# A two-block transformer kernel: small parameter loads put behind the first layer's weights

## The reference, cut to what matters

```python
a = rms_norm(h, attn_norm[i])
proj = a @ w_in[i]                       # queries, keys, values, z, xbc, dt, ...
(da_q, da_k, da_v, ssd_z, ssd_xbc, ssd_dt, gla_q, gla_k, gla_v, gla_g, gla_lr) = jnp.split(proj, IN_SPLITS, axis=-1)
y_da  = diff_attention(da_q, da_k, da_v, positions, da_q_norm[i], da_k_norm[i], ...)
y_ssd = ssd_mixer(ssd_z, ssd_xbc, ssd_dt, ssd_conv_w[i], ssd_conv_b[i], ...)   # xbc is convolved over 4 tokens
y_gla = gla_mixer(gla_q, gla_k, gla_v, gla_g, gla_lr, gla_w_gate2[i], gla_b_gate[i], gla_norm[i])
h = h + concat(y_da, y_ssd, y_gla) @ w_out[i]
f = rms_norm(h, ffn_norm[i])
h = h + (silu(f @ w_ffn_gate[i]) * (f @ w_ffn_up[i])) @ w_ffn_down[i]
h = h + sigmoid(h @ ple_w_gate[i]) * (p[i] @ ple_w_proj[i])
# the second block's modulation, computed during the first block's layers:
mod = silu(c) @ ada_w[i] + ada_b[i]      # and its norm gains norm_pre, norm_post, mla_qa_norm
```

## Time and profile before

| | |
|---|---|
| median of three runs | 1738.55 us |
| the profiled execution's own time | 1739.91 us |
| its span in the profile | 1737.8 us |
| TensorE multiplying | 1689.4 us, 97% of the span |
| VectorE busy | 1185.4 us, 68% |
| ScalarE busy | 905.2 us, 52% |
| GpSimd busy | 41.9 us, 2% |

### The profile page before, as it was taken

One profiled execution on the slowest core, in us unless ns is written; L12 is line 12 of the kernel. 1 busy time (PEld: TensorE's weight loads), 2 busy tenths in 40 slices (PEclk: granted clock), 3 DMA queues, 4 the chain that ended last, 5 costly groups with the idle time before them and its releaser, 6 DMA issues.

```text
span 1737.8 us, 34117 instructions
## 1 busy us (share of the span) xinstructions
PE 1689.4 (97%) x14251; PEld 1462.7 (84%) x14251; DVE 1185.4 (68%) x1656; ACT 905.2 (52%) x1124; POOL 41.9 (2%) x50
## 2 busy tenths in 40 slices
PE   6999999998999999999999999999999989999998
PEld 5977899987987799988888888888888878898896
DVE  4888755537588765546567877768677683687875
ACT  5666433335575443335645545456455562465772
POOL 2000000000000000000000000000000000000130
PEclk9999999999999999999999999999999999999999
DMA  7666778653648756655222322313223123352022
GB/s 199 197 221 257 223 179 200 193 192 130 196 155 306 244 160 181 192 194 170 77 86 62 98 62 62 94 54 98 62 62 98 51 98 134 116 188 79 26 72 99
DMA packets 252857, 241.90 MB, mean 139 GB/s; under 512 B 32932, under 2 KB 212224, under 8 KB 252064
## 3 DMA queue, kind: packets, MB, share of 16 engines
q1 hardware_dynamic: 250896, 233.21, 43.4%
q0 software_dynamic: 1808, 6.50, 1.3%
HBM read 238.61 MB, written 1.08 MB: 138 GB/s over the span
## 4 chain that ended last, share of the span: by engine, by line
PE 82%; DVE 7%; ACT 4%; DMA 3%; DVEq 2%; issue 1%; ACTq 1%; SPq 1%
PE pg L2653 35%; PE pg L1315 34%; PE pm L1315 7%; PE pm L1318 2%; PE pm L2653 2%; DVE ring_r L576 2%; PE pm L2656 1%; DMA ring<-in_w_ffn_up 1%; DVE ring_r L1762 1%; ACT ring_r L569 1%; SPq L2221 1%; DMA ring<-in_hg_w_in 1%; DVEq L1799 1%; DMA ring<-in_w_in 0%; DMA cst<-in_cst 0%
## 5 line engine op out<-in xcount | busy, mean ns | idle before, releaser
L576 DVE TENSOR_TENSOR ring_r<-ring,ring_r 128x2048 fp32r<-128x2048 f32 (+1 forms) x126 | 284.2, 2261 | 170.0 <-ACT ring_r L569 163.8
L2653 PE MATMUL pg<-ring_r,work_r 128*128 128x512 f32 (+1 forms) x1632 | 375.7, 389 | 8.6 <-DVEq L3172 2.7
L2653 PEld LDWEIGHTS pg<-ring_r,work_r 128*128 128x128 f32 x1632 | 299.0, 189 | 77.2 <-issue 10.2
L1315 PE MATMUL pg<-ring_r,work_r 128*128 128x512 f32 (+3 forms) x1280 | 354.6, 383 | 5.5 <-DVE work_r L1768 1.5
L569 ACT ACTIVATE ring_r<-ring 128x2048 fp32r<-128x2048 f32 (+1 forms) x126 | 237.5, 1890 | 200.7 <-DMA ring<-in_w_ffn_up 80.6
L2653 PE MATMUL pg<-work_r,ring_r 128*128 128x256 f32 x2688 | 318.8, 281 | 1.7 <-DVE ring_r L576 1.6
L2653 PEld LDWEIGHTS pg<-work_r,ring_r 128*128 128x128 f32 x2688 | 317.2, 188 | 3.3 <-DVE ring_r L576 2.4
L1315 PE MATMUL pg<-ring_r 128*128 128x512 f32 (+3 forms) x752 | 284.2, 378 | 1.1 <-DVEq L831 1.1
L1315 PEld LDWEIGHTS pg<-ring_r,work_r 128*128 128x128 f32 x1280 | 235.5, 188 | 50.2 <-DVEq L1763 3.5
L1315 PE MATMUL pg<-work_r,ring_r 128*128 128x512 f32 (+1 forms) x976 | 264.4, 360 | 0.0
L1315 PEld LDWEIGHTS pg<-work_r,ring_r 128*128 128x128 f32 x976 | 173.1, 189 | 27.2
(11 more groups left out here) (401 smaller groups left out, 1808.3 us busy)
## 6 DMA issues: line engine op xcount, KB each, us to landing
ring<-in_w_in SPq DMA_DIRECT2D x36, 1024.0 KB, 5.3
ring<-in_hg_w_in SPq DMA_DIRECT2D x48, 512.0 KB, 3.9
ring<-in_w_ffn_gate SPq DMA_DIRECT2D x44, 512.0 KB, 4.0
ring<-in_w_ffn_up SPq DMA_DIRECT2D x44, 512.0 KB, 5.4
ring<-in_w_ffn_down SPq DMA_DIRECT2D x22, 1024.0 KB, 4.9
ring<-in_ada_w SPq DMA_DIRECT2D x16, 1024.0 KB, 8.9
ring<-in_hg_w_in SPq DMA_DIRECT2D x64, 256.0 KB, 3.0
ring<-in_w_out SPq DMA_DIRECT2D x12, 1024.0 KB, 5.7
```

The costliest lines, as they stand in the source:

```text
L576: W.low_done(V.tensor_tensor(lo, W.raw(i, name)[:, 0:lo.shape[1]], W.hi(i, name).bitcast(f32), ALU.subtract))
L1315: return T.matmul(out_, lhsT, rhs, start=first, stop=last)
L2653: return T.matmul(out_, lhsT, rhs, start=first, stop=last)
```

## The change

The convolution's bias and filters move from ahead of piece 4 to behind it, and the row loads move ahead of it. The second norm's gain and the modulation's bias leave the small loads (22 become 20) and are issued behind the layer's last weight piece, on the semaphore of the second half of x, for which ScalarE and VectorE wait ahead of the second norm. GpSimd's five gains of the second block move behind its loads for the first layer.

```diff
-        N_PRM = 22
+        N_PRM = 20
...
                 small_loads = [
-                    (p_convb, cols("ssd_conv_b", i)),
                     (p_qkg[:, 0:DQK], rows("da_q_norm", i)), (p_qkg[:, DQK:], rows("da_k_norm", i)),
...
-                    (p_dskip, rows("ssd_d", i)), (p_ssdn, rows("ssd_norm", i)), (p_glan[:, 0:1], cols("gla_norm", i)),
-                    (p_sub[:, 0:1], cols("da_sub_norm", i)),
-                    (p_ffn, cols("ffn_norm", i)), (p_li, d["lam"][i]),
-                    (p_adab, d["ada_b_2"][i].rearrange("(c p) -> p c", p=P)),
+                    (p_dskip, rows("ssd_d", i)), (p_convb, cols("ssd_conv_b", i)),
                 ]
-                for j in range(4):
-                    small_loads.insert(1 + j, (convw3[:, j, :], d["ssd_conv_w"][i, j].rearrange("(c p) -> p c", p=P)))
+                small_loads += [(convw3[:, j, :], d["ssd_conv_w"][i, j].rearrange("(c p) -> p c", p=P)) for j in range(4)]
+                small_loads += [(p_ssdn, rows("ssd_norm", i)), (p_glan[:, 0:1], cols("gla_norm", i)),
+                                (p_sub[:, 0:1], cols("da_sub_norm", i)), (p_li, d["lam"][i])]
...
+            def load_late_parameters(i):
+                sp.wait_ge(loaded_h[1], 16 + 32 * i)
+                sp.dma_start(p_ffn, cols("ffn_norm", i)).then_inc(loaded_h[1], 16)
+                sp.dma_start(p_adab, d["ada_b_2"][i].rearrange("(c p) -> p c", p=P)).then_inc(loaded_h[1], 16)
...
-            for k, (a, b) in enumerate(((0, 12), (12, 16), (16, N_PRM))):
+            for k, (a, b) in enumerate(((0, 11), (11, 16), (16, N_PRM))):
                 load_parameters(first_loads[a:b])
                 load_w_in(0, w_in_pieces[4 + k:5 + k])
             for i in range(DEPTH):
                 load_w_in(i, w_in_pieces[4 if i else 7:])
+                if i == 0:
+                    load_late_parameters(0)
...
                     if next_loads and j == 16:
                         e_gu.wait(sp, i, 4)
-                    if 6 <= j < 17:
+                        load_late_parameters(i + 1)
+                    if 6 <= j < 16:
                         load_parameters(next_loads[2 * (j - 6):2 * (j - 5)])
...
-            second_pool_early(pool)
             for i in range(DEPTH):
...
+                if i == 0:
+                    second_pool_early(pool)
...
                 e_pp.set(act.drain())
+                act.wait_ge(loaded_h[1], 16 + 32 * i + 32)
                 norm1_high(p_ffn, A_LATER[0])
...
                 low(gu_pieces[1])
+                dve.wait_ge(loaded_h[1], 16 + 32 * i + 32)
                 norm1_low(p_ffn, A_LATER)
```

More of the change, by code:

```diff
@@ L579, in program @@
         cum_store = nc.dram_tensor("cum_store", (16, P), f32).ap()
-        loaded_const, loaded_h = sem("const_loaded"), [sem("h_loaded"), sem("h_second_loaded")]
+        loaded_const, loaded_h = sem("const_loaded"), [sem("h_loaded"), sem("h_second_and_late_params_loaded")]
         loaded_attn, loaded_prm, loaded_p = sem("attn_norm_loaded"), sem("params_loaded"), sem("p_loaded")
-        N_PRM = 22
+        N_PRM = 20
         sin_in, sin_out = sem("sin_arguments"), sem("sin_done")
```

## The result

The changed kernel took 1741.28 us (median of 17 runs, 1739.89 to 1745.07), the kernel before, in turns with it on the same chip, 1738.72 (17 runs, 1736.5 to 1741.55): a ratio of 1.0015, with a 95% interval of 1.0009 to 1.0022. It is slower by 2.6 us. The forecast was 1736.6, and its range ended at 1740.4. The profiled execution's span is 1739.5 us, where that of before is 1737.8.

A forecast was written before the change was run, and what follows sets the result against it. TensorE bounds the kernel (82% of the chain); late weight pieces cost the first layer 2.1 us. xbc1 1.98 earlier gives 1737.9 profiled; with the runs' median 1.4 below the profiled execution, 1736.6 us, range 1733.9 to 1740.4.

The forecast's parts named there:

- Moved on GpSimd: Five gains behind the cumulative rows' broadcast: about 0.51 us per 1024 features, falling where SyncE's pieces wait for TensorE; no cost.
- The two loads behind the last piece of w_in: Second norm's gain and modulation's bias, issued later on SyncE: wanted only at about 205 us, so no cost.
- Piece 4: First half of xbc0's weights: landing at 33.4 to 34.7 instead of 36.8, removing TensorE's 1.57 us wait before xbc0.
- Rival (a): Small loads did not make xbc0's first weight piece late; it still lands at 36.8, time 1738.1 us; chance 0.12.
- Piece 5: xbc0's second weight piece behind five column loads: issue 32.3 to 37.3, early half taken, landing about 40.0, 0.9 us spare.
- rival (c): Five columns on SyncE's queue hold the next weight pieces: 0.8 to 2.3 us slower, 1739.3 to 1740.9; chance 0.11.
- The term: Start of the first layer's convolved columns: xbc1 starts at 50.81 in place of 52.79, a gain of 1.98 us.
- Piece 6: xbc1's first weight piece: issued about 39.7, landing 45.6, needed by 46.5; issue bounds 36 and 44.9.
- The two added waits: On ScalarE and VectorE ahead of the second norm: long fulfilled, cost nothing; uncovered some 0.05 us each.
- the second layer: Small loads change order inside its gate and up loop, where TensorE waits for no piece: no cost.
- a gain is kept: After 64.20 everything follows TensorE; VectorE still waits 2.44 us at 108.20, so the 1.98 gained fits.

The follow-up runs named there:

- run 3: Changed kernel with the second norm's gain and modulation's bias behind four pieces of output weights (about 160 us), five gains kept at 115 us: 1741.16 us, 1.0012 of before.
- run 9: Changed kernel with two of GpSimd's five gains left at 115 us and the other three moved to about 210 us: 1737.72 us, 0.9997 of the kernel before.
- run 1: Changed kernel with GpSimd's five gains put back in their old place, ahead of its loads for the first layer: 1739.74 us, 1.0005 of the kernel before.
- run 2: Changed kernel with GpSimd's five gains moved behind the second norm, about 210 us, the next layer's gain going along: 1737.9 us, 0.9997 of before.
- run 4: Changed kernel with the five gains at about 210 us and the second norm's gain and modulation's bias at about 160 us: 1739.02 us, 1.0001 of before.
- run 5: Kernel before with only GpSimd's five gains moved to about 210 us, the next layer's gain going along: 1738.01 us, 0.9993 of the kernel before.

## Why the prediction was wrong

**"Moved on GpSimd: ... Neither costs anything that I can find": this is the step that failed**, and with it the sign. I priced the five loads nearly rightly, at "0.51 us or so" for 1024 features: runs 3 and 9 have 0.6 to 0.7. But I let them fall "where SyncE's next pieces wait for TensorE". SyncE does wait for TensorE's slots there, until 114.88 for one pair of pieces and until 120.46 for the next. But these are the modulation's four, and once issued they fill the DMA engines to a share of 1.02 until the product that wants them at 128, with 0.8 to 0.9 us to spare. I had named 128 as a place to look for a new wait, and had read no row of that stretch. Measured: 1.77 with the gains there and the late parameters away, 2.98 with both, nothing with the gains at 210 (runs 1 to 4). I had also seen only five loads: the sixth, the next layer's gain, is pushed among the weights by them.

**The two loads behind the last piece of w_in** I held against their use at 205 alone. Their 4096 columns drain ahead of `cum_store`, on whose landing GpSimd waits to issue the broadcast: 1.4 us longer (3.12 to 4.56). Without the gains that costs 0.27 (run 1) or nothing (run 2). With them the difference of two single traces is 1.2 (2.98 - 1.77), which the spread of the fourth piece's landing in traces without any gains, 8.8 to 10.0, doesn't let me call theirs.

**Piece 4: right in the wait of 1.57 that it removes.** It landed 6.4 after its issue, at 35.3, and not by 34.7, since its slot came free 0.5 later; TensorE, later by as much, wanted it by 35.5 (39.86 - 4.3). Rival (a) fell. But I had named two causes, and they count unequally: the piece lands 8.4 after its issue before, 7.4 with the edits on SyncE's queue alone (run 1), 6.6 with the gains alone away (run 5), 6.4 with both. The gains are enough to remove the wait, the columns on SyncE's queue are not: with them gone and the gains in place 0.58 of the 1.57 stays. Whether it is the gains' own packets or those of p, which was issued 4 us later behind them, no run separates.

**Piece 5: the wrong half of the bounds.** I put its issue at 32.3 to 37.3 and took the early half; it was 36.37, and it landed at 42.7, not 40.0. This is rival (c)'s mechanism, just below the landing of 42.9 from which (c) was to decide. The 1.70 for a column load behind a megabyte was the nearer row than the 3.10 for four on an empty queue. The term gave 0.70 in place of 1.98 (0.73 to 1.33 of wait ahead of piece 5 in the runs that keep this order). I also wrote that this wait would stand behind the 96th product; piece 5 begins behind the 48th.

**Piece 6: right in its issue, by luck** (39.80 for "about 39.7"), and it landed at 47.0 for 45.6. The forecast had taken two issues off its way and left the rest. In fact piece 5 was issued 4.2 later than before, and the SSD gain, 3.74 before, took 0.58 behind it: the two bounds that I had named, 36 and 44.9, came true together and nearly cancelled. Behind the new wait TensorE wanted xbc1 only at 47.00 + 5.65 = 52.65, so that was 1.3 early enough. That its small loads had to leave for it was wrong: with only the gains gone it was issued at 37.91 (run 5).

**The two added waits, the second layer, and that a gain is kept**: nothing in the traces speaks against them. Of the 3.0 lost by 209.85 the last products of the program show 1.7 (1728.90 to 1730.60 in single executions), the medians 2.6; the 1.3 between goes in steps of 0.2 to 0.4, at about 600, 970, 1040, 1120 and 1260, so I take it for scatter, without having shown it.

So 0.7 came in where 2.0 was forecast, and 3.0 went out where nothing was.

## What to carry to other kernels

A small load that is moved off one critical load has to be costed at the place where it lands, in the DMA engines' share there, on every queue and not only on that of its engine: ask which transfers run then and how much they have to spare, before asking when the load itself is wanted. What stands behind a moved load or a new wait moves too, and belongs in the sum. Column loads belong where no transfer is awaited; on a queue that must issue the next weight piece they are worst, since they hold the issue. And where one edit of several carries the suspicion, cost it alone: here one edit of the change, the five gains, held all of the gain by the place that they left, and most of the loss by the place that they went to (all of it that single traces let me tell from scatter).

## What the hardware showed that I had not expected

A column load of 1024 features is recorded as some thousand packets on SyncE's queue (3088 packets, 0.02 MB, in 2 us) but as a few dozen on GpSimd's (195 for most of the six loads around 120 us). Its cost to a stream beside it is much the same: 0.6 to 0.7 us for 1024 features there, by the landing of the fourth piece, and 0.51 to 0.66 (2000 in one microsecond, 3088 in two) where hardly anything else ran. The share of the engines that its queue is given in the profile (10.7%) says little of that cost; the lengthened packets of the other queue (0.278 us for 0.153) say it.

How long SyncE needs to issue a column load depends on what is in its queue: 0.58 to 1.81 for the first behind a megabyte, 5.5 to 7.4 for the four filters after it, 5.62 for one in the worst place. Most row loads take 0.34 to 0.6, but they can be held as well: 1.59 behind the four filters before the change (22.37), and 3.74 for the SSD gain behind piece 5.
